# Convolution states of a trunk-layer kernel: turned by VectorE's 32 by 32 transpose and stored by eight DMAs, in place of 24 TensorE transposes and two DMAs

## The reference, cut to what matters

```python
def causal_conv(u, past, w):
    S = u.shape[1]
    upad = jnp.concatenate([past.astype(u.dtype), u], axis=1)
    out = upad[:, 0:S] * w[0]
    for j in range(1, CONV_W):
        out = out + upad[:, j:j + S] * w[j]
    return jax.nn.silu(out), upad[:, upad.shape[1] - (CONV_W - 1):]     # the second value is the state
...
u, z, a, b, cq, ckv, kpe = jnp.split(h @ p['w_in'], idx, axis=-1)
uc, conv_new = causal_conv(u, conv_past, p['conv_w'])
...
o_mla = block_causal_attention(q * (QK_DIM ** -0.5), k_mla, v_mla, q_pos, k_pos)
x = x + mix @ p['w_out']
...
x = x + moe_ffn(h, w_router, b_router, w_gu, b_gu, w_down, b_down)      # 32 experts, 12.6 MB of weights each
```

## Time and profile before

| | |
|---|---|
| median of 3 runs | 1329.73 us (1329.09 to 1329.92) |
| the profiled execution | 1326.95 us, span 1325.1 us |
| TensorE matmul busy | 1277.6 us, 96% of the span |
| VectorE / ScalarE / GpSimd busy | 459.1 / 214.7 / 19.5 us |
| read from HBM | 436.62 MB |

### The profile page before, as it was taken

The page is one execution under the profiler, slowest core; times in us unless marked ns, Lnnn a source line. Parts: engine busy times, 40 slices in busy tenths (PEclk is TensorE's granted clock), DMA queues, the critical chain, the costliest instruction groups (busy, mean ns, idle before and its releaser), DMA issues.

```text
span 1325.1 us, 21045 instructions
## 1 busy us (share of the span) xinstructions
PE 1277.6 (96%) x8616; PEld 582.0 (44%) x8616; DVE 459.1 (35%) x977; ACT 214.7 (16%) x573; POOL 19.5 (1%) x28
## 2 busy tenths in 40 slices
PE   5899999999999999999999999999999999999997
PEld 4567645567655333343333343333333333333332
DVE  2354334532655233332233332233332233332223
ACT  3452233650341000000000000000000000000000
POOL 0000001200000000000000000000000000000000
PEclk9899999999998999999999999999999999999999
DMA  9511210663218999999999999999999999999996
GB/s 336 215 58 30 106 29 16 232 220 152 80 64 352 428 427 427 428 429 428 428 429 428 428 429 429 429 428 429 428 427 430 428 429 428 429 428 428 429 428 267
DMA packets 48046, 440.53 MB, mean 332 GB/s; under 512 B 7635, under 2 KB 10169, under 8 KB 23334
## 3 DMA queue, kind: packets, MB, share of 16 engines
q1 hardware_dynamic: 47916, 439.90, 79.9%
q10 hardware_dynamic: 90, 0.06, 0.0%
HBM read 436.62 MB, written 3.33 MB: 332 GB/s over the span
## 4 chain that ended last, share of the span: by engine, by line
PE 75%; DMA 16%; SPq 3%; DVE 3%; ACT 2%; issue 1%; POOL 0%; DVEq 0%
PE bank L1052 73%; DMA weights<-in_w_gu 15%; SPq L419 3%; PE bank L1055 2%; DMA gain_cols<-in_norm_ffn 1%; ACT scaled L613 1%; POOL stats L585 0%; PE bank L1690 0%; DVE weights L1816 0%; DVE x L2380 0%; DVE x L2229 0%; ACT stream L613 0%; DVE stats L2159 0%; DVE stream L1816 0%; DVE x L1816 0%
## 5 line engine op out<-in xcount | busy, mean ns | idle before, releaser
L2380 DVE SCALAR_TENSOR_TENSOR x<-bank,small_weights,x 128x512 f32<-128x512 f32 (+1 forms) x192 | 134.8, 743 | 598.4 <-PE bank L1052 598.4
L1052 PE MATMUL bank<-weights,small_weights 128*64 128x512 f32 (+4 forms) x1456 | 336.0, 588 | 3.1 <-DMA weights<-in_w_gu 3.1
L1052 PEld LDWEIGHTS bank<-weights,small_weights 128*64 128x64 f32 (+1 forms) x1456 | 105.7, 139 | 195.5 <-issue 171.6
L1052 PE MATMUL bank<-weights,scaled 128*64 128x512 f32 x704 | 155.9, 595 | 5.1 <-ACT scaled L613 5.1
L613 ACT ACTIVATE scaled<-bank 128x256 f32<-128x256 f32 (+5 forms) x153 | 58.2, 408 | 323.9 <-PE bank L1052 241.8
L1052 PE MATMUL bank<-scaled,small_weights 64*128 64x512 f32 x384 | 108.1, 640 | 1.4 <-DVE x L2380 0.7
L613 ACT ACTIVATE scaled<-scaled 128x512 f32<-128x512 f32 x32 | 20.1, 629 | 549.6 <-DVE scaled L1820 549.6
L1052 PE MATMUL bank<-stream,small_weights 128*64 128x512 f32 (+4 forms) x408 | 89.5, 547 | 2.4 <-ACT small_weights L613 1.3
L1052 PEld LDWEIGHTS bank<-weights,scaled 128*64 128x64 f32 x704 | 48.7, 137 | 97.1 <-issue 87.8
L1052 PE MATMUL bank<-small_weights 96*64 96x512 bf16 (+2 forms) x408 | 86.6, 496 | 0.9 <-DVE small_weights L1816 0.9
L1052 PE MATMUL bank<-small_weights,weights 128*128 128x320 f32 (+3 forms) x320 | 86.6, 420 | 0.7 <-ACT small_weights L613 0.7
(11 more groups left out here) (193 smaller groups left out, 907.3 us busy)
## 6 DMA issues: line engine op xcount, KB each, us to landing
weights<-in_w_gu SPq DMA_DIRECT2D x85, 2048.0 KB, 26.8
weights<-in_w_down SPq DMA_DIRECT2D x44, 2048.0 KB, 28.1
stream<-in_w_gu SPq DMA_DIRECT2D x21, 2048.0 KB, 27.9
more_weights<-in_w_gu SPq DMA_DIRECT2D x11, 2048.0 KB, 27.5
small_weights<-in_w_gu SPq DMA_DIRECT2D x11, 2048.0 KB, 26.0
small_weights<-in_w_down SPq DMA_DIRECT2D x10, 2048.0 KB, 28.0
more_weights<-in_w_down SPq DMA_DIRECT2D x10, 2048.0 KB, 28.3
weights<-in_w_in SPq DMA_DIRECT2D x4, 2048.0 KB, 14.4
```

What stands on the lines that cost most here:

```text
L1052: return pe.matmul(out, lhsT, rhs, start=start, stop=stop)
L2380: dve.scalar_tensor_tensor(xx, PS[bank][0:rows, :], gcur[0:rows, b:b + 1], xx, ALU.mult, ALU.add)\
```

## The change

The copies of `convolve` now write `ulast` in W2, [128, s, j, 32 columns], of which column f is filled and the rest set to zero at the start. Behind the last convolution's copies VectorE transposes the six blocks of 32 columns, in each quarter of the partitions by itself, so that partition 32q + f holds 32 features in a row for each s and j. The SyncE queue stores these by eight DMAs, each of 12 partitions by 3 by 32 elements (36 runs of 128 bytes), waits for them, and only then loads slot 8, which lies over them. The TensorE transposes, ScalarE's copies, `cs_out`, the two stores and the waits for them are gone.

```diff
-        ulast = SM[:, 84:156].rearrange("p (f s j) -> p f s j", f=NU, s=2)
+        ulast = W2[:, 0:192].rearrange("p (s j f) -> p s j f", s=2, f=32)
+        ulastT = W2[:, 192:384].rearrange("p (s j i) -> p s j i", s=2, i=32)
...
             load(wmv_sb, k_major(w_mv[0], 0, KD), "ld_wmv")
+            sp.wait_ge(sem("cs_ready"), 1)
+            for s, dst in enumerate((p_conv, s_conv)):
+                by_row = dst[0, 0].rearrange("j (f q i) -> q f j i", q=4, i=32)
+                for q in range(4):
+                    sp.dma_start(by_row[q], ulastT[32 * q:32 * q + NU, s, :, :]).then_inc(sem("st_conv"), 16)
+            sp.wait_ge(sem("st_conv"), 128)
             first_tiles(SLOTN - 1, SLOTN)
...
-            sp.wait_ge(sem("cs_ev"), 6)
-            sp.dma_start(p_conv[0, 0], cs_out[:, 0, :]).then_inc(sem("st_conv"), 16)
-            sp.dma_start(s_conv[0, 0], cs_out[:, 1, :]).then_inc(sem("st_conv"), 16)
             sp.wait_ge(sem("xT_tr"), KD)
...
-            sp.wait_ge(sem("st_conv"), 32)
             sp.wait_ge(sem("st_mk"), 32)
...
-                if CS_AT <= n < CS_AT + 6:
-                    i = n - CS_AT
-                    act.wait_ge(sem("cs_tr"), i + 1)
-                    run(cs_out[:, i // 3, 512 * (i % 3):512 * (i % 3) + 512], PS[6 + i % 2][0:3, :]).then_inc(sem("cs_ev"), 1)
...
-                if CS_AT <= n < CS_AT + 6:
-                    i = n - CS_AT
-                    if i >= 2:
-                        pe.wait_ge(sem("cs_ev"), i - 1)
-                    for f in range(4):
-                        m = tr(PS[6 + i % 2][0:3, f * P:(f + 1) * P], ulast[:, 4 * (i % 3) + f, i // 3, :])
-                    m.then_inc(sem("cs_tr"), 1)
                 if XT_AT <= n < XT_AT + KD:
                     k = n - XT_AT
                     if k == 0:
                         pe.wait_ge(sem("ld_x"), 64)
-                    if k < 2:
-                        pe.wait_ge(sem("cs_ev"), 5 + k)
-                    else:
+                    if k >= 2:
                         pe.wait_ge(sem("xT_ev"), 2 * (k - 2) + 1)
...
+            dve.memset(ulast, 0.0)
...
-                dve.tensor_copy(ulast[:, f, 0, :], upad[:, f, SEQ:SEQ + 3])
-                dve.tensor_copy(ulast[:, f, 1, :], upad[:, f, T + 3:T + 6])
+                dve.tensor_copy(ulast[:, 0, :, f], upad[:, f, SEQ:SEQ + 3])
+                m = dve.tensor_copy(ulast[:, 1, :, f], upad[:, f, T + 3:T + 6])
+                if i == NU - 1:
+                    link(m)
+                    dve.transpose(W2[:, 192:384], W2[:, 0:192]).then_inc(sem("cs_ready"), 1)
```

More of the change, by code:

```diff
@@ L252, in trunk_kernel @@
         qmT = R[:, 2432:3712].rearrange("p (h t) -> p h t", h=H)
-        cs_out = W[0:3, 13312:16384].rearrange("p (s n) -> p s n", s=2)
         wmq_sb = W[:, 0:4096].rearrange("p (k n) -> p k n", k=KD)
@@ L359, in trunk_kernel @@
                                   [vm[:, i, h * P:(h + 1) * P] for i in range(2)], om[:, h, qs]))
-        CS_AT, XT_AT = 2, 7
+        XT_AT = 7
         KVB = [(4, 6), (5, 7), (0, 1), (4, 7), (5, 6)]
@@ L571, in _ @@
                 sp.wait_ge(sem("st_out"), 16 * (3 * TB))
-            for name, n in (("st_state", 2), ("st_lat", 4), ("st_conv", 2), ("st_mk", 2), ("st_out", 2 * TB)):
+            for name, n in (("st_state", 2), ("st_lat", 4), ("st_conv", 8), ("st_mk", 2), ("st_out", 2 * TB)):
                 sp.wait_ge(sem(name), 16 * n)
```

## The result

The changed kernel is slower: 1335.11 us (median of 7 runs, 1332.51 to 1337.17) against 1329.09 (7 runs, 1326.81 to 1329.92), ratio 1.0049, 95% interval 1.0037 to 1.0061. The forecast was no change, 1329.7 us in a range up to 1331.8.

A forecast was written before the change was run, and what follows sets the result against it. The experts' flat tile stream, started by the first refill at 411.65 us, was taken to set the end. Removal -0.04, VectorE 0 and SyncE queue 0 left the base of 1329.73 at 1329.7 us, range 1327.4 to 1331.8.

The forecast's parts named there:

- What bounds the kernel: Experts end with a flat-rate tile stream, started by the first refill at 411.65 us; only savings reaching that refill count.
- The removal: Six groups of TensorE transposes and six ScalarE copies in the MLA attention go: -0.04 us, from -0.08 to 0.
- The first group: Step 2's four transposes, ahead of a TensorE wait that does not depend on them: worth nothing.
- the five others: Remaining transpose groups, up to step 7: at most 5 x 0.43 = 2.15 us, a lead lost again in step 8.
- the wait at 259.6: TensorE idle for 1.11 us at 259.64 while VectorE normalizes a key block; makes the transposes ahead of it worth nothing.
- the rival of the clock: Clock falls behind step 8's new TensorE wait: 1.7 us slower, 1331.4 us; chance 0.3.
- the new wait of step 8: TensorE, 2.15 us early at 270.54, stands still some 2.1 us, until about 272.65, for ScalarE's copy.
- the outer case: Clock stays low as long as in 394 to 406: 5.2 us slower, 1334.9 us; chance beyond the bound 0.05.
- The wait for w_mq: ScalarE stops in step 7 until this load lands, delaying the copy TensorE needs in step 8; takes back the 2.15 us.
- VectorE's transpose: Ahead of the last convolution: 0.4 us taken with the round trip, 2.3 us of delay covered, price 0.
- the moved stores: Eight SyncE issues, 4 us, to about 133; 48 us free before the store at 188.63; price 0.
- slot 8: Its load starts at 140 instead of 128.77; it holds a second-expert tile computed after 411.65; price 0.

The follow-up runs named there:

- e5: Changed kernel with the TensorE transpose groups of steps 3 to 7 put back on other data, not the first group: 1331.08 us, ratio 1.0020.
- e1: Changed kernel with all six groups of TensorE transposes put back at their old places, on other data: 1329.57 us, ratio 1.0011.
- e4: Changed kernel with three matmuls of constants ahead of the key block wait in step 3 of the MLA attention: 1327.71 us, ratio 0.9995.
- e7: e4 with ScalarE's multiplication of w_mq moved behind its other work of each step: 1326.26 us, ratio 0.9992 to the kernel before.
- The square: Table of e1, e2, e5 and the changed kernel, by first group and groups of steps 3 to 7 there or left out: 1.0011, 1.0040, 1.0020, 1.0049.
- e2: Changed kernel with only the first of the six transpose groups (step 2) put back on TensorE, on other data: 1334.44 us, ratio 1.0040.

## Why the prediction was wrong

**What bounds the kernel: right.** The experts run off the flat stream of tiles, and in all twelve profiles the end came 913 to 915 us after the first refill. One reading was off by a slice: the flat rate begins with the fourteenth (428 GB/s), the thirteenth has 352.

**The removal: the step that failed.** "The first group ... is worth nothing" and the price of the five others took TensorE's work for time only. It also helped to hold the clock up. Without the groups the clock fell at the wait at 259.6 and did not come back for 23.9 us (the windows after); with only the later ones in place it came back after 3.4 us (e5); with all in place it did not fall there (e1). With the wait filled by other work it did not fall either, and the loss was gone (e4, 0.9995). The same mistake sits in the choice of place: the rival of the clock was put behind the new wait of step 8, and it fell 13 us ahead of that, at a wait the prediction had on its list and had closed as having no price. In the changed kernel the wait of step 8 never came about, since TensorE at half clock was no longer early.

**The size given to that rival** was 1.7 us, with up to 5.2 us as the outer case (1334.9 us) and 0.05 for it. Both were taken from falls that were followed by dense work (x2, the experts). The row that should have been read beside them is the attention itself: short products with waits in between, which had been at 1.00 all along but gave no evidence of being able to raise a clock that had fallen. The loss in the profile was 8.7 us there, and 6.0 us between the medians. That this row was the one to read is argued from the result, not tested. That the outer case, 1334.9, is 0.2 us from the measured 1335.11 is luck: its length came from the routers, and the place was another.

**The wait for w_mq: right**, by its mechanism and nearly by its size, once the clock is kept: 1.73 us of TensorE waiting in e4 where 2.1 were forecast, gone in e7 when ScalarE's order was changed.

**VectorE's transpose, the moved stores, slot 8: right.** 0.38 us where 0.4 was taken; the slot's load at 138.28 where 140 was; the next store at 188.59. e1 keeps all three and stands at 1.0011 (0.9998 to 1.0024).

**The weight given to a rule on transposes.** The prediction drew on the Trainium skill, "TensorE: Matmul & The Clock Gate", section "Part 4: PE-mode transpose", by which a transpose in TensorE's transpose mode does not count as busy in the same way; from that it let the removed groups count for nothing. The square says otherwise for these: only transposes (stationary 128 x 3, 128 columns moving) tell e5 from the changed kernel, and with them the clock was low for 3.4 instead of 23.9 us, and the ratio 1.0020 instead of 1.0049. The measurement decides. Whether they are of the kind that the Trainium skill's page means, and whether they act as work or by the time that they take between other rows, is not known from the runs. The fall of 286 to 290, which the prediction took as agreeing with this rule, followed steps that held products beside their transposes; it can't tell the two apart.

**What stays open.** By what the groups hold the clock up was not measured. Nor is it known what makes one execution of e2 fall (1342.58 us) and another not (1327.38 us).

## What to carry to other kernels

Before TensorE work is taken out of a stretch of short, dependent steps, read PEclk there and ask what holds it up; the price of a removal is then not only its duration but, where the work behind it does not bring the clock back, up to half of the time that the clock then stays low (8.7 of 23.9 us here). Compare the mean clock of every run and not one profile alone. A few matmuls of constants in TensorE's waits are a cheap test: where they make the kernel faster and the profile shows the clock kept, the low clock had cost time.

## What was not expected of the hardware

- The clock can stay at 1.2 GHz for 23.9 us, with TensorE shown busy in all but the first 0.6 us of it (259.1 to 283.0 of the changed kernel), although it had run the same kind of steps at 2.4 GHz.
- Adding TensorE work to a path that it sets itself made the kernel faster: three matmuls of about 0.5 us each in the last steps kept the clock through 276 to 290 in the profile, where e7 had a mean of 0.53 over 11 us, and with them the median went from 0.9992 to 0.9976 of before.
- The same program takes from 1327.4 to 1342.6 us (e2); of what is recorded of each execution only the mean clock (0.990 to 0.977) goes with it.
